# Reordering the prologue of a two-layer diffusion backbone: first modulation tile ahead of x, conditioning rows spread by TensorE, narrow products sooner

## The chip, the cores and the metric

The kernel runs on one core of one Trainium2 chip. The metric is the time of one execution on the device in microseconds, as the median of several runs. All data is fp32 unless said otherwise; "fp32r" is the form of fp32 operands for which TensorE needs one pass over the columns.

## The reference

512 tokens (256 context, 256 latent) of width 1024 go through two layers, each with a SwiGLU FFN, a token mixer and a second FFN. Ahead of each of these stands an adaptive norm. Only the first of them is touched by the change:

```python
s_lat = jax.nn.silu(c)                 # (1, 1024), conditioning of the latent tokens
s_ctx = jax.nn.silu(c_ctx)[None]       # (1, 1024), of the context tokens
m = s @ ada_w[l] + ada_b[l]            # 9 vectors of 1024: shift, scale, gate for three sub-layers
h = rms_norm(x, g) * (1 + scale) + shift
g, u = jnp.split(h @ w_in, 2, axis=-1)
y = (jax.nn.silu(g) * u) @ w_out
```

The scale and shift of the first norm are needed before the first product of the first FFN can run; every later modulation vector is made beside the FFN products.

## The kernel before

Tokens lie along the free axis: `x` is 128 partitions by 8 chunks (KD = 8) of the width by 512 tokens. A weight tile of 128x2048 is fetched raw, ScalarE copies its rounded half (`split_hi`, L463), VectorE subtracts to get the rest (`split_lo`, L684), and every product is three one-pass matmuls: low times high, high times low, high times high (`products`, L1025 to L1027). Each engine has one program written out in order; semaphores join them. SyncE (`sp_program`) issues the large loads on one queue, GpSimd (`pool_program`) the small tables and later the modulation tiles, ScalarE the first tables.

The prologue is what runs before the first FFN is in its stride. In the order of the code:

- SyncE issues the conditioning columns `c_cols` (8 KB), four loads of `x` (512 KB each, two chunks each), weight tile 0 (1 MB), `ada00` tile 0 (1 MB; tile k holds in its first half the weights of scale chunk k and in its second those of shift chunk k), `c_ctx` and `c` each broadcast to 128 partitions (512 KB each, into `silu_c`), `ada00` tile 1, weight tile 1, then `ada00` tiles 2 to 7.
- GpSimd waits for `ada00` tile 0, then issues eight small tables (semaphore `loaded`, 8 loads), then waits for `ada00` tile 7 and begins with the modulation tiles of the later norms.
- TensorE runs 20 filler matmuls on a zero tile (`idle`, 128x512 bf16, L1128), adds up the squares of x in four steps (L1289, two chunks each) with three fillers after each, spreads the inverse root over the partitions (`pe_rstd`, L1271), and enters `pe_first_pairs`. There `narrow(n, w)` multiplies tile n's scale (w = 0) or shift (w = 1) half by `c_cols`: 8 matmuls of 2 columns, 16 instructions (L1135). Chunk 0 takes both halves this way; for chunks 1 to 7 only the scale is made so (`scale(n)`), and the shift is made on VectorE by `dots(n)`: two multiply-and-sum instructions of 128x1024 (L947), one per stream.
- `main(k, s)` is the part of the first two output tiles (s = 0, 1) that chunk k of the normalised input gives: 6 matmuls of 128x512. From chunk 1 on TensorE's order is `main(k, 0)`, `main(k, 1)`, `scale(k + 2)`.
- ScalarE (`act_modulate`, `one(c)`) makes scale (L595) and shift (L599) of chunk c, applies them (L605, two streams) and rounds (L610). VectorE multiplies x by the inverse root (`rows`, L939) and makes the low half (`low`, L952).
- ScalarE needs a table of functions per kind. Before, it has the one for Sqrt loaded first and the one for Silu after the root of the first norm; Silu is next used at L475 in the first FFN.

## Time and profile before

| what | value |
|---|---|
| median of 3 runs | 2031.32 us |
| lowest, highest | 2025.6, 2032.45 us |
| span of the profiled execution (its own time, first to last instruction) | 2029.5 us |
| TensorE matmul busy | 1988.7 us, 98% |
| TensorE busy in the first 65 us | 62.46 us |
| mean granted TensorE clock, first 65 us | 0.89 |
| mean granted TensorE clock, whole span | 0.989 |
| share of the 16 DMA engines, first 65 us | 0.75 |

TensorE is busy nearly throughout, but in the prologue its busy time holds fillers, narrow matmuls whose time is their weight load, and stretches at half clock. The granted clock of 1 stands for 2.4 GHz, 0.5 for 1.2 GHz. The record of the clock begins at 1.00, but the fillers of the first microseconds stand 0.43 us apart, twice the 0.21 of later ones, so durations are the better witness there.

### The profile page before, as it was taken

To read this page: it belongs to the slowest core of one execution; us is meant where nothing else is said; L and a number is where in the kernel's file an instruction comes from. 1 tells how busy PE (TensorE), PEld (TensorE's weight loads), DVE (VectorE), ACT (ScalarE), POOL (GpSimd) and SP (SyncE) were. 2 spreads that over 40 slices of the span, in tenths; PEclk is the share of its full clock that TensorE was granted. 3 is DMA by queue.
4 is the path that set the end of the run, shared out by engine and by line. 5 is a ranking of instruction groups with operands and counts; after the bars stand their busy time and mean duration, and the time that the engine had idled before them with its cause. 6 is when DMAs were issued, how large, how long until landed. Compare 5 with 4: busy or idle time off the path is not lost.

```text
span 2029.5 us, 27640 instructions
## 1 busy us (share of the span) xinstructions
PE 1988.7 (98%) x10255; PEld 1686.5 (83%) x10255; DVE 1282.1 (63%) x1840; ACT 752.0 (37%) x990; POOL 109.0 (5%) x165
## 2 busy tenths in 40 slices
PE   9999999999999899999999999999999999989998
PEld 7888888896788889888888988888887888878886
DVE  6877577875647776877678753453346632656666
ACT  4422222345544334332122333212235432736453
POOL 1000000000003210000001000000000000000000
PEclk8999999999999999999999999999999999999999
DMA  9455555621220003555555532352234423043553
GB/s 350 165 184 179 176 188 173 198 94 42 83 73 21 1 11 115 192 181 182 177 184 169 180 125 96 101 176 96 68 127 147 151 97 104 21 161 135 177 191 124
DMA packets 52650, 274.80 MB, mean 135 GB/s; under 512 B 6128, under 2 KB 7472, under 8 KB 34256
## 3 DMA queue, kind: packets, MB, share of 16 engines
q1 hardware_dynamic: 33024, 203.97, 28.7%
q0 software_dynamic: 18960, 68.88, 10.2%
q8 instruction: 63, 1.03, 0.2%
q10 hardware_dynamic: 576, 0.69, 0.1%
q14 instruction: 27, 0.22, 0.0%
HBM read 272.47 MB, written 1.05 MB: 135 GB/s over the span
## 4 chain that ended last, share of the span: by engine, by line
PE 90%; DVE 4%; ACT 3%; DMA 1%; issue 1%; SPq 0%; DVEq 0%; ACTq 0%
PE ps L1025 15%; PE ps L1026 15%; PE ps L1027 15%; PE ps L1037 8%; PE ps L1255 6%; PE ps L1257 6%; PE ps L1256 6%; PE ps L1038 4%; PE ps L2402 2%; PE ps L2404 2%; PE ps L2403 2%; PE ps L1907 1%; DMA ada<-in_ada 1%; PE ps L1919 1%; PE ps L2488 1%
## 5 line engine op out<-in xcount | busy, mean ns | idle before, releaser
L684 DVE TENSOR_TENSOR w_lo<-w_raw,w_hi 128x2048 fp32r<-128x2048 f32 (+3 forms) x206 | 420.8, 2043 | 198.0 <-ACT w_hi L463 197.4
L1025 PE MATMUL ps<-h_parts,w_lo 128*128 128x512 f32 (+1 forms) x1424 | 537.5, 377 | 1.5 <-DVE w_lo L684 0.6
L1026 PE MATMUL ps<-h_parts,w_hi 128*128 128x512 f32 (+1 forms) x1424 | 534.9, 376 | 0.0
L1027 PE MATMUL ps<-h_parts,w_hi 128*128 128x512 f32 (+1 forms) x1424 | 534.9, 376 | 0.0
L463 ACT ACTIVATE w_hi<-w_raw 128x2048 fp32r<-128x2048 f32 (+3 forms) x207 | 354.0, 1710 | 444.8 <-PE ps L1257 254.0
L692 DVE SCALAR_TENSOR_TENSOR ada_product<-ada_w,silu_c 128x1024 bf16<-128x1024 f32 x256 | 313.2, 1224 | 20.4 <-DVE ada_product L692 10.3
L1025 PEld LDWEIGHTS ps<-h_parts,w_lo 128*128 128x128 f32 x1424 | 268.8, 189 | 51.2 <-DVE h_parts L2240 1.1
L1027 PEld LDWEIGHTS ps<-h_parts,w_hi 128*128 128x128 f32 x1424 | 268.8, 189 | 48.7
L1026 PEld LDWEIGHTS ps<-h_parts,w_hi 128*128 128x128 f32 x1424 | 268.8, 189 | 47.5
L475 ACT ACTIVATE sil<-ps 128x512 f32<-128x512 f32 x66 | 39.5, 598 | 481.1 <-PE ps L1027 481.1
L1255 PE MATMUL ps<-hid_parts,w_lo 128*128 128x512 f32 x468 | 182.1, 389 | 0.0
L1256 PE MATMUL ps<-hid_parts,w_hi 128*128 128x512 f32 x468 | 182.1, 389 | 0.0
L1257 PE MATMUL ps<-hid_parts,w_hi 128*128 128x512 f32 x468 | 182.1, 389 | 0.0
L717 DVE TENSOR_TENSOR prod<-sil,ps 128x512 f32<-128x512 f32 x66 | 45.4, 688 | 184.7 <-ACT sil L475 184.7
L1037 PE MATMUL ps<-h_parts,w_hi 128*128 128x512 f32 x416 | 149.0, 403 | 2.6 <-DVE h_parts L901 2.4
L755 DVE SCALAR_TENSOR_TENSOR x<-ps,mod,x 128x256 f32 (+1 forms) x144 | 65.4, 481 | 114.9 <-PE ps L1257 90.9
L428 POOL DMA_DIRECT2D ada_w<-in_ada x128 | 67.6, 529 | 964.3 <-DVE ada_product L692 936.3
L1038 PE MATMUL ps<-h_parts,w_lo 128*128 128x256 f32 x416 | 117.4, 282 | 0.0
L1257 PEld LDWEIGHTS ps<-hid_parts,w_hi 128*128 128x128 f32 x468 | 87.9, 188 | 18.3
L1256 PEld LDWEIGHTS ps<-hid_parts,w_hi 128*128 128x128 f32 x468 | 87.9, 188 | 18.2
L1255 PEld LDWEIGHTS ps<-hid_parts,w_lo 128*128 128x128 f32 x468 | 87.9, 188 | 18.2
L1037 PEld LDWEIGHTS ps<-h_parts,w_hi 128*128 128x128 f32 x416 | 79.4, 191 | 23.0 <-issue 2.6
(337 smaller groups left out, 2547.9 us busy)
## 6 DMA issues: line engine op xcount, KB each, us to landing
w_raw<-in_w_up SPq DMA_DIRECT2D x88, 1024.0 KB, 4.8
ada_w<-in_ada POOLq DMA_DIRECT2D x128, 512.0 KB, 3.5
w_raw<-in_w_down SPq DMA_DIRECT2D x32, 768.0 KB, 4.2
w_raw<-in_w_down SPq DMA_DIRECT2D x32, 640.0 KB, 3.9
w_raw<-in_w_ret_t SPq DMA_DIRECT2D x16, 1024.0 KB, 4.8
w_raw<-in_w_ab SPq DMA_DIRECT2D x14, 1024.0 KB, 4.7
ada<-in_ada SPq DMA_DIRECT2D x8, 1024.0 KB, 26.9
w_raw<-in_w_ret SPq DMA_DIRECT2D x8, 1024.0 KB, 4.7
```

Of the source, the lines that this page charges most:

```text
L428: pool.dma_start(ada_w[:, slot, :], a["ada"][bass.ds(index, 1)].rearrange("a p n -> (a p) n")) \
L463: act.activation(w_hi[parts_of(s, slot)][:, 0:elems], w_raw[slot][:, 0:elems], ACT.Copy).then_inc(hi_ready, 1)
L684: dve.tensor_tensor(w_lo[parts_of(s, slot)][:, 0:elems], w_raw[slot][:, 0:elems], w_hi[parts_of(s, slot)][:, 0:elems].bitcast(F32), ALU.su ...
L692: dve.scalar_tensor_tensor(out=ada_product[:], in0=ada_w[:, slot, :], scalar=1.0, in1=silu_c[:, st, :], op0=ALU.mult, op1=ALU.mult, accum_ ...
L1025: pe.matmul(out, lo, rhs_hi(k), start=first and k == 0, stop=False)
L1026: pe.matmul(out, hi, rhs_lo(k), start=False, stop=False)
L1027: mm = pe.matmul(out, hi, rhs_hi(k), start=False, stop=last and k == nk - 1)
L1037: pe.matmul(out, w_hi[slot][:, off:off + P], parts, start=start, stop=stop, skip_group_check=True)
L1038: return pe.matmul(out[:, LAT], w_lo[slot][:, off:off + P], parts[:, 1], start=False, stop=stop, skip_group_check=True)
L1255: pe.matmul(ps[:, 2 * slot, cols], wlo, hi, start=k == 0, stop=False)
L1256: pe.matmul(ps[:, 2 * slot, cols], whi, lo, start=False, stop=False)
L1257: mm = pe.matmul(ps[:, 2 * slot, cols], whi, hi, start=False, stop=k == nk - 1)
```

## The change

- SyncE: `ada00` tile 0 is issued ahead of the four loads of x; the two broadcasts of `c_ctx` and `c` go away.
- ScalarE: fetches `c_ctx` and `c` as rows of one partition (two loads, ahead of its tables), takes Silu of the columns and of the rows first, then squares, and runs the warm-up Sqrt after the squares.
- TensorE: 12 fillers, `narrow(0, 0)`, 3 fillers, `narrow(0, 1)`, 3 fillers ahead of the sums of squares; no filler between or after these. Four matmuls of 128x512 with a one-partition operand (`pe_spread_c`) spread the two Silu rows into PSUM banks 0 to 3: one before the third sum, one after the fourth, two after `pe_rstd`. VectorE copies the context row from PSUM into `silu_c`, ScalarE the latent row.
- The shift of chunk 1 is made by a narrow product too (`TURNED = 2`), so `dots` starts at chunk 2. The order in `pe_first_pairs` becomes `narrow(1, 0)`, `main(0, 0)`, `narrow(1, 1)`, `scale(2)`, `main(0, 1)`; its 14 fillers go away.
- VectorE: `low(0)` comes ahead of the copy, and later the order is `rows(c)`, `dots(c)`, `low(c - 1)`.
- GpSimd issues the small tables after `ada00` tile 6 instead of tile 0.

```diff
@@ sp_program
         sp.dma_start(c_cols, a["c_cols"]).then_inc(c_cols_loaded, 16)
+        scale_and_shift(0)
         for i in range(KD // 2):
             sp.dma_start(x[:, 2 * i:2 * i + 2], a["xT"][:, 2 * i:2 * i + 2]).then_inc(x_loaded[i], 16)
         weights(0)
-        scale_and_shift(0)
-        sp.dma_start(silu_c[:, 0, :], a["c_ctx"].partition_broadcast(P)).then_inc(c_loaded, 16)
-        sp.dma_start(silu_c[:, 1, :], a["c"][0, :].partition_broadcast(P)).then_inc(c_loaded, 16)
         scale_and_shift(1)
@@ pool_program
-        pool.wait_ge(ada00_ready[0], 16)
+        pool.wait_ge(ada00_ready[KD - 2], 16)
@@ act_modulate
-                if c:
-                    act.wait_ge(first_dot, 2 * c)
-                act.activation(mod[:, 0, 1, :, c], mcol[:, :, c] if c else ps[:, 5, 2:4], ACT.Identity,
+                if c >= TURNED:
+                    act.wait_ge(first_dot, 2 * (c - TURNED + 1))
+                act.activation(mod[:, 0, 1, :, c], ps[:, 5 + c % 2, 2:4] if c < TURNED else mcol[:, :, c], ACT.Identity,
...
                 if c == 0:
+                    act.wait_ge(c_spread, 2)
+                    act.activation(silu_c[:, 1, :].rearrange("p (b n) -> p b n", b=2), ps[:, 2:4, :], ACT.Copy) \
+                       .then_inc(c_spread_lat, 1)
                     split_hi(act, 1, 1, ELEMS[1])
@@ scalar_program
+        for st, row in enumerate((a["c_ctx"].unsqueeze(0), a["c"])):
+            act.dma_start(silu_c[0:1, st, :], row).then_inc(c_loaded, 16)
         act.dma_start(const[:, 0:2 * P], a["const"][:, 0:2 * P]).then_inc(const_loaded, 16)
...
-        act.wait_ge(sem("eps_set"), 1)
-        act.activation(warm_root[:], vecs[:, 2:3], ACT.Sqrt).then_inc(warmed, 1)
+        act.wait_ge(c_cols_loaded, 16)
+        act.activation(c_cols, c_cols, ACT.Silu).then_inc(c_silu, 1)
+        act.wait_ge(c_loaded, 32)
+        act.activation(silu_c[0:1], silu_c[0:1], ACT.Silu).then_inc(c_silu, 1)
         for r in range(0, KD, 2):
             act.wait_ge(x_loaded[r // 2], 16)
             act.activation(first_squares[:, r], x[:, r], ACT.Square).then_inc(even_squared, 1)
+        act.wait_ge(sem("eps_set"), 1)
+        act.activation(warm_root[:], vecs[:, 2:3], ACT.Sqrt).then_inc(warmed, 1)
         act_root(act, "n00", 0, 1.0 / D)
-        act.wait_ge(c_cols_loaded, 16)
-        act.activation(c_cols, c_cols, ACT.Silu).then_inc(c_silu, 1)
         split_hi(act, 0, 0, ELEMS[0])
-        act.wait_ge(c_loaded, 32)
-        act.activation(silu_c[:], silu_c[:], ACT.Silu).then_inc(c_silu, 1)
@@ vector_program
         rows(0)
+        split_lo(dve, 0, 0, ELEMS[0])
+        low(0)
+        dve.wait_ge(c_spread, 1)
+        dve.tensor_copy(silu_c[:, 0, :].rearrange("p (b n) -> p b n", b=2), ps[:, 0:2, :]).then_inc(c_spread_ctx, 1)
         rows(1)
-        split_lo(dve, 0, 0, ELEMS[0])
-        dve.wait_ge(c_silu, 2)
-        dots(1)
-        low(0)
         split_lo(dve, 1, 1, ELEMS[1])
-        for c in range(2, KD):
-            if c > 2:
-                dots(c)
-            low(c - 1)
-            if c == 2:
-                dots(c)
-            rows(c)
+        rows(2)
+        dve.wait_ge(c_spread_ctx, 1)
+        dots(2, (0,))
+        low(1)
+        dve.wait_ge(c_spread_lat, 1)
+        dots(2, (1,))
+        for c in range(3, KD):
+            rows(c)
+            dots(c)
+            low(c - 1)
@@ pe_spread_c, pe_first_pairs
+    def pe_spread_c(pe, st, half):
+        return pe.matmul(ps[:, 2 * st + half, :], one_column[0:1, 0:1].to_broadcast([1, P]),
+                         silu_c[0:1, st, half * 512:(half + 1) * 512], start=True, stop=True)
...
             if k == 0:
                 pe_ready(pe, s)
+                pe.wait_ge((c_spread_ctx, c_spread_lat)[s], 1)
...
-        narrow(0, 0)
-        idle(pe, 4)
-        narrow(0, 1).then_inc(scale_made, 1)
-        idle(pe, 4)
-        scale(1)
+        narrow(1, 0)
         main(0, 0)
-        idle(pe, 4)
+        narrow(1, 1).then_inc(scale_made, 1)
         scale(2)
-        idle(pe, 2)
         main(0, 1)
@@ tensor_program
-        idle(pe, 20)
+        idle(pe, 12)
+        pe.wait_ge(c_silu, 1)
+        pe_narrow(pe, 0, 0)
+        idle(pe, 3)
+        pe_narrow(pe, 0, 1).then_inc(scale_made, 1)
+        idle(pe, 3)
         for i in range(KD // 2):
+            if i == 2:
+                pe.wait_ge(c_silu, 2)
+                pe_spread_c(pe, 0, 0)
             pe.wait_ge(pair_summed, i + 1)
...
-            idle(pe, 3)
+        pe_spread_c(pe, 0, 1).then_inc(c_spread, 1)
         pe.wait_ge(const_loaded, 16)
         pe_rstd(pe, "n00", 0)
-        idle(pe, 3)
+        pe_spread_c(pe, 1, 0)
+        pe_spread_c(pe, 1, 1).then_inc(c_spread, 1)
```

The host side lays the shift half of `ada00` tile 1 out in columns like that of tile 0, at the same size.

## Rows read from the trace of the kernel before

**Rows 1.** The page's first line.

```profile
span 2029.5 us, 27640 instructions
```

**Rows 2.** The chain that ended last, first 70 us: shares by line; pieces (start, us, what).

```profile
by line: DMA ada<-in_ada 34.0%; PE ps L1135 14.8%; PE ps L1025 12.3%; PE ps L1026 11.0%; PE ps L1027 10.6%; SPq L387 2.5%; issue 1.7%; SPq L380 1.6%; ACT sil L605 1.6%; SPq L390 1.4%; SPq L383 1.4%; DVE h_parts L952 1.0%; DVE prod L717 1.0%
...
7.06 23.78 DMA ada<-in_ada
```

**Rows 3.** TensorE in order of time (start us, us, line, what, count).

```profile
1.48 7.02 PE L1128 MATMUL ps<-idle_tile 128*128 128x512 bf16 x20 [1.48 <-DVE idle_tile L923]
...
12.74 0.95 PE L1289 MATMUL ps<-one_column,first_squares 128*128 128x1 f32 x8
...
14.35 1.13 PE L1271 MATMUL ps<-const,small 128*128 128x128 f32 x8
...
15.96 1.85 PE L1135 MATMUL ps<-small,ada 128*128 128x2 f32 x16
...
22.56 3.57 PE L1135 MATMUL ps<-small,ada 128*128 128x2 f32 x16 [0.49 <-DMA ada<-in_ada]
...
28.71 1.93 PE L1128 MATMUL ps<-idle_tile 128*128 128x512 bf16 x4
30.89 1.95 PE L1135 MATMUL ps<-small,ada 128*128 128x2 f32 x16 [0.25 <-DMA ada<-in_ada]
...
32.93 0.58 PE L1025 MATMUL ps<-h_parts,w_lo 128*128 128x512 f32 x1
...
38.84 1.84 PE L1135 MATMUL ps<-small,ada 128*128 128x2 f32 x16
...
43.41 1.84 PE L1135 MATMUL ps<-small,ada 128*128 128x2 f32 x16
```

**Rows 4.** Two stretches: busy us by engine, granted clock (PEclk), DMA share, GB/s.

```profile
20.00:22.00 2.00, 2.00 (x8) 0.62 (x7) 0.00 (x0) 1.69 (x5) 0.43 (x1) 0.57 1.02 389
30.00:32.00 2.00, 1.75 (x12) 1.12 (x11) 2.00 (x3) 0.21 (x1) 0.00 (x0) 0.87 1.02 430
```

**Rows 5.** DMA issues of single stretches: KB, us from issue to landing.

```profile
x<-in_xT SPq DMA_DIRECT2D x1, 512.0 KB, 6.4
...
w_raw<-in_w_up SPq DMA_DIRECT2D x1, 1024.0 KB, 10.0
...
w_raw<-in_w_up SPq DMA_DIRECT2D x1, 1024.0 KB, 19.5
...
small<-in_lam POOLq DMA_DIRECT2D x1, 128.0 KB, 11.7
```

**Rows 6.** VectorE in order of time.

```profile
11.64 0.69 DVE L929 TENSOR_TENSOR first_squares<-first_squares 128x512 f32<-128x512 f32 x1
...
15.51 1.28 DVE L939 TENSOR_TENSOR prod<-x,ps 128x512 f32<-128x512 f32 x2 [1.26 <-PE ps L1271]
17.35 2.29 DVE L684 TENSOR_TENSOR w_lo<-w_raw,w_hi 128x2048 fp32r<-128x2048 f32 x1 [0.55 <-ACT w_hi L463]
```

**Rows 7.** ScalarE in order of time.

```profile
20.49 0.35 ACT L595 ACTIVATE mod<-ps,mod_tmp,norm_g 128x2 f32<-128x2 f32 x1 [0.27 <-PE ps L1135]
...
22.15 0.63 ACT L610 ACTIVATE h_parts<-sil 128x512 fp32r<-128x512 f32 x1
...
63.91 0.60 ACT L475 ACTIVATE sil<-ps 128x512 f32<-128x512 f32 x1 [2.53 <-PE ps L1027]
```

**Rows 8.** Later TensorE matmuls with two-pass fp32 operands of 512 columns.

```profile
479.28 1.13 PE L1405 MATMUL ps<-df 64*128 64x512 f32 x4
```

**Rows 9.** One line: a VectorE copy of 128x1024 from PSUM, ns min/median/max.

```profile
L2333 DVE COPY df<-ps x4: 1219/1222/1225, 425.0 to 452.5; 128x1024 f32<-128x1024 f32 x4
```

**Rows 10.** ScalarE later, a table load and the activation behind it.

```profile
527.00 1.28 ACT L1696 ACT_TABLE_LOAD   x1
531.22 0.31 ACT L1696 ACTIVATE small<-small,vecs 128x16 f32<-128x16 f32 x1 [2.94 <-DVE small L1700]
```

**Rows 11.** GpSimd in order of time.

```profile
43.71 1.06 POOL L428 DMA_DIRECT2D ada_w<-in_ada  x2 [23.28 <-DMA ada<-in_ada]
```

More of the change, by code:

```diff
@@ L939, in rows, with dots @@
             dve.tensor_tensor(prod[:, c % 2], x[:, c], ps[:, NRM, :], ALU.mult).then_inc(normed, 1)
-        def dots(c):
+        def dots(c, streams=range(2)):
             dve.wait_ge(ada00_ready[c], 16)
-            for st in range(2):
-                n = 2 * (c - 1) + st
+            for st in streams:
+                n = 2 * (c - TURNED) + st
                 if n:
@@ L1128, in idle, with pe_narrow @@
             pe.matmul(ps[:, 7, :], idle_tile[:, 0:P], idle_tile[:], start=True, stop=True)
+    def pe_narrow(pe, n, w):
+        if w == 0:
+            pe.wait_ge(ada00_ready[n], 16)
+        for k in range(KD):
+            mm = pe.matmul(ps[:, 5 + n % 2, 2 * w:2 * w + 2], first_weights(n)[:, w, k * P:(k + 1) * P],
+                           c_cols[:, 2 * k:2 * k + 2], start=k == 0 and w == 0, stop=k == KD - 1,
+                           skip_group_check=True)
+        return mm
+    def pe_spread_c(pe, st, half):
+        return pe.matmul(ps[:, 2 * st + half, :], one_column[0:1, 0:1].to_broadcast([1, P]),
+                         silu_c[0:1, st, half * 512:(half + 1) * 512], start=True, stop=True)
     def pe_first_pairs(pe):
         def narrow(n, w):
-            for k in range(KD):
-                mm = pe.matmul(ps[:, 5 + n % 2, 2 * w:2 * w + 2], first_weights(n)[:, w, k * P:(k + 1) * P],
-                               c_cols[:, 2 * k:2 * k + 2], start=k == 0 and w == 0, stop=k == KD - 1,
-                               skip_group_check=True)
-            return mm
+            return pe_narrow(pe, n, w)
         def scale(n):
-            pe.wait_ge(ada00_ready[n], 16)
-            if n >= 2:
-                pe.wait_ge(first_mod, n - 1)
+            pe.wait_ge(first_mod, n - 1)
             narrow(n, 0).then_inc(scale_made, 1)
```

8 lines of the change are left out of this document (4 added, 4 removed).

## Prediction

> **What bounds the kernel now.** The page gives a span of 2029.5 us [rows 1]; the median of the runs is 2031.32 us, 1.8 us more. I make the sum on the profiled execution and subtract the result from the median. The runs shown scatter over 6.9 us (2025.6 to 2032.45), so 0.3% (6.1 us) is about what a measurement can tell from no change.
>
> I read the chain of waits first. In its first 70 us the largest share, 34%, is one transfer: `ada00` tile 2, issued at 7.06 and landed 23.78 us later, at 30.85 [rows 2]. `scale(2)` starts on TensorE right then, at 30.89 [rows 3]. Next I read TensorE in order of time. After `scale(2)` come `main(0, 1)` at 32.93, then 18 matmuls of 128x512 in all, then `scale(3)` at 38.84. From there on a period of 4.57 us (38.84 to 43.41) repeats with hardly a gap [rows 3]: 16 instructions of a narrow product and 12 wide matmuls. So the prologue is bound by a transfer up to 30.9 us and by TensorE's own work after it. Whatever brings the start of `scale(3)` forward brings the end forward by the same, because the work behind it is unchanged. **38.84 us is the mark to beat.**
>
> The third thing to see is the clock. The same 16 instructions of a narrow product take 1.85 us at 15.96 and 3.57 us at 22.56; four fillers take 1.93 us at 28.71 (0.43 each), where 12 cold and 8 warm ones fill the first 7.02 us: 12 x 0.43 = 5.1, 8 x 0.21 = 1.7 and the tail of the last [rows 3]. The granted clock agrees: its mean over 20 to 22 us is 0.57, so it fell to 0.5 early in that stretch, and over 30 to 32 us it is 0.87, so it came back [rows 4]. It fell after two narrow products with four fillers between; it came back after 6 wide matmuls and 4 fillers in a row. Prices below are written "at 2.4 | at 1.2 GHz".
>
> **The change, part by part.** *Ahead of the sums.* Twelve fillers from 1.48 last 12 x 0.43 = 5.1, to 6.6. Then TensorE waits for `ada00` tile 0. It is now the first megabyte of the queue. Before, the first megabyte was the first two loads of x; the second of them was issued at about 1.8 and landed 6.4 later, at 8.2 [rows 5]. The start therefore lies between 6.6 and 8.2; I take the middle, 7.4. ScalarE's Silu of the columns (a table load of 1.28 [rows 10], and a few tenths) is done by about 5, under the fillers. Two narrow products at 1.84 and six fillers at 0.21 make 5.0, so the sums can start at 12.4.
>
> *Sums of squares and spreads.* x lies a megabyte later in the queue. Its last load now ends where weight tile 0's third megabyte ended: issued 3.29, landed 10.0 later, 13.3 [rows 5]. VectorE then needs two passes of 0.69 [rows 6], to 14.7, which is before TensorE reaches the fourth sum. So TensorE is late, not x: four sums at about 1.0 (0.95 busy [rows 3]), with one spread in between. The trace has no matmul of 512 columns with one partition. From below it is bounded by the one-pass wide matmul, 0.23; from above by the two-pass fp32 matmuls of 512 columns over half the rows, four instructions in 1.13 [rows 8], if none of them overlap, 0.57 for two. The two-pass instructions of 512 columns at filler rate give 4 x 0.21 = 0.85 if each instruction streams its columns twice, and this is the bound I take, since it is the dearest. Sums end at 12.4 + 4.0 + 0.85 = 17.3. Before they ended at 12.74 + 0.95 = 13.7 [rows 3]: 3.6 later. The next spread (0.85) hides root and inverse, which took 0.7 between 13.7 and 14.35; then `pe_rstd` takes 1.1 [rows 3], to 19.3 (before 15.5).
>
> *Up to `main(0, 0)`.* VectorE: `rows(0)` 0.64, `split_lo` 2.29 [rows 6], by then ScalarE has rounded chunk 0 (20.49 to 22.78, 2.3 in all [rows 7], here 19.9 to 22.2), `low(0)` 0.69, and the new copy from PSUM 1.22 [rows 9]. That is 4.9 with the small overlaps: 24.2. TensorE meanwhile does two spreads and `narrow(1, 0)`: 19.3 + 1.7 + 1.84 = 22.8, covered; if VectorE's 4.9 were gone, it would be the bound 1.4 earlier. The copy is on the path, since `main(0, 0)` writes the banks it reads. Before, `main(0, 0)` started behind the narrow product of 22.56, at 26.1 [rows 3].
>
> *Up to `main(0, 1)`.* Six matmuls 1.4 | 2.6 and two narrow products 3.7 | 6.9 [rows 3]: 5.1 | 9.5, so 29.3 | 33.7. The same kinds of work ran mostly at 1.2 GHz in the stretch this replaces. I take the middle, 31.5, against 32.93. Tile 2 is now the seventh megabyte; the seventh before, weight tile 1, was issued at 6.59 and landed 19.5 later, at 26.1 [rows 5], and it had the small tables beside it, which are now moved behind. `scale(2)` asks for it at 27.4 at the earliest, so it is no longer waited for. ScalarE's copy (about 1.1) and split of weight tile 1 and VectorE's part of it end near 27.5, covered.
>
> *Up to `scale(3)`.* 18 matmuls: 4.2 all at 2.4 GHz; before 38.84 - 32.93 = 5.9, part of it at 1.2. I take 5.9: 31.5 + 5.9 = 37.4. **Sum: 38.84 - 37.4 = 1.4 us gained.** At the fast ends 29.3 + 4.2 = 33.5, a gain of 5.3; VectorE's new order (copy, `rows(1)`, `split_lo(1)`, `rows(2)`, `dots(2)`, `low(1)`, `rows(3)`, `dots(3)`, `low(2)`) reaches 35.4 there, when TensorE has done `scale(3)` at 35.3, so it does not cut this. At the slow ends 33.7 + 5.9 = 39.6, a loss of 0.8.
>
> *Edits costed at nothing.* `dots(1)` leaves VectorE, 2.5 us that did not set the end. VectorE's work per chunk, 0.65 + 2.5 + 0.69 = 3.8, stays under TensorE's 4.57. GpSimd's tables: even if issued from 43.7 [rows 11], eight at 0.54 and the slowest landing of 11.7 [rows 5] give 59.7, before the end of the last chunk at about 62; their real start is tile 6, earlier. If that margin went, all three engines would stand at `loaded`. The modulation tiles queue behind them on GpSimd by 4.3 us; nothing reads them before the first FFN. The third table load: Silu's table must come back before L475. A table load ran ahead of its activation's wait at 527.00 (end 528.28, then 2.94 idle [rows 10]), and L475 has 2.53 of idle [rows 7], so 1.28 is hidden; unhidden it costs 1.3.
>
> The Trainium skill, "ScalarE: Activation LUTs", section "What ACT_TABLE_LOAD costs", puts a switch at about 2.66 us with its drain. The trace shows 1.28 and an activation right behind; by the page the load at L475 would stick out of its cover by 0.1 us.
>
> **The rivals.** *B, the clock falls in the first narrow products and stays down through the sums.* For it: the pair narrow, fillers, narrow is what stood ahead of the fall at 20 us, and now there are 3 fillers instead of 4 between, a wait ahead of it, and none between the sums. Against it: the sums before, with three fillers after each, and the narrow product at 15.96 behind them ran at the prices of 2.4 GHz [rows 3], and the spreads are dense work in the fillers' place. Price, with narrow's ratio 3.57/1.85 for work set by weight loads: fillers 0.65, sums 4 x 0.9 = 3.7, two spreads 1.7, `pe_rstd` 0.9: 7.0, so `pe_rstd` ends at 26.3, and TensorE's two spreads and `narrow(1, 0)` at 1.2 GHz (3.4 + 3.4) end at 33.1, past VectorE. Then 5.1 | 9.5 and 5.9 give 44.1 to 48.5: 5.3 to 9.7 slower, **2036.6 to 2041.0 us**. It decides the sign as soon as it costs over 1.4 us, that is from two cold sums on, and passes 0.3% at 7.5.
>
> The Trainium skill, "TensorE: Matmul & The Clock Gate", section "What's actually happening", says that the array is throttled by default and that activity releases it; the rows of the clock agree, and by this rule leaving 18 of the 49 fillers speaks for B.
>
> *C, the queue is no faster.* If tile 2 still lands at 30.9, because the large loads and not the small tables slowed the queue, `scale(2)` ends at 32.7 and `main(0, 1)` starts 0.2 earlier: **2031.1 us**. For it: the DMA engines are full (share 1.02) in both stretches [rows 4]. Against it: the queue carries one megabyte less ahead of tile 2.
>
> *D, the clock holds throughout:* gain 5.3, **2026.0 us**. For it: the sums' stretch before. Against it: the narrow products do not hold it.
>
> **How the numbers follow.** The forecast (A, partly cold) gets 0.47, B 0.22, C 0.13, D 0.12, and 0.06 is for what lies elsewhere. A: 2031.32 - 1.4 = **2029.9 us**, its own range 2026 to 2032. The range over all is 2025.0 to 2039.0: from D's 2026.0 with a microsecond of scatter to the middle of B; outside are B's upper part and scatter. Faster by over 0.3% needs D and scatter: 0.08. Slower by over 0.3%: three quarters of B, and a little for the rest: 0.18. Within: 0.74.
>
> **What the profile after would show.** The first narrow product at 6.6 to 8.2 us; sums ending near 17.3, `pe_rstd` near 19.3, a copy of 1.22 on VectorE ending just ahead of `main(0, 0)` near 24.2; `scale(2)` without a wait for DMA; `scale(3)` near 37.4; a table load inside the idle time ahead of L475. B shows as narrow products of 3.4 us or sums of 1.8 before 20 us and a granted clock of 0.5 there. C shows as a DMA wait at `scale(2)`. If the spreads take far from 0.85 each, or the first tile lands after 8.2, that term is wrong; if `scale(3)` moves and the span doesn't, the step that carries the prologue's gain to the end is.

## The result and the profile after

The changed kernel takes 2042.29 us, the median of 9 runs from 2036.9 to 2043.4. The kernel before, run 9 times beside it, takes 2026.62 us (2022.69 to 2032.45). The ratio is 1.0061 with a 95% interval of 1.0049 to 1.0073. The two medians alone differ by 15.7 us (0.77%), the ratio stands for 12.3 us; the ratio with its interval is what is used from here on. The change makes the kernel slower by about 0.6%, and the time lies above the stated range, though the kernel before turned out 4.7 us faster in nine runs than in the three that the forecast was subtracted from. One execution of the kernel before, in the group of experiment 10, took 6544.77 us and is left out of the ratios. The profiled execution took 2042.18 us.

The page's first line stands against [rows 1]: the span grew by 10.9 us.

```profile
span 2040.4 us, 27627 instructions
```

The chain of waits of the changed kernel, its first pieces (start us, us, what), answers to [rows 2]. The one long transfer is gone. From 6.71 us on, with hardly a gap, every piece up to the first FFN is TensorE.

```profile
1.34 5.24 DMA ada<-in_ada
6.71 1.98 PE ps L1144 x16
8.70 1.30 PE ps L1136 x3
10.00 3.20 PE ps L1144 x16
13.20 1.30 PE ps L1136 x3
14.51 3.21 PE ps L1306 x16
17.71 2.00 PE ps L1150 x2
19.71 3.50 PE ps L1306 x16
23.21 2.00 PE ps L1150 x2
25.21 2.00 PE ps L1280 x8
27.21 3.71 PE ps L1150 x4
30.92 3.50 PE ps L1144 x16
```

In the changed file L1144 is the narrow product, L1136 a filler, L1306 the sum of squares, L1150 the spread of a conditioning row, L1280 `pe_rstd`, and L1033 to L1035 the three wide matmuls. Two instructions of L1150 are one spread and 16 of L1306 are two sums.

TensorE of the changed kernel in order of time, behind the last piece above, answers to [rows 3]. The 16 instructions at 50.53 are `scale(3)`, which started at 38.84 before: **11.7 us later**. The one at 78.36 is the first of the third weight tile, which started at 65.38 before: 13.0 us later.

```profile
34.28 0.77 PE L1033 MATMUL ps<-h_parts,w_lo 128*128 128x512 f32 x1
...
36.99 6.82 PE L1144 MATMUL ps<-small,ada 128*128 128x2 f32 x32
43.67 0.77 PE L1033 MATMUL ps<-h_parts,w_lo 128*128 128x512 f32 x1
...
50.53 1.84 PE L1144 MATMUL ps<-small,ada 128*128 128x2 f32 x16
...
55.10 1.84 PE L1144 MATMUL ps<-small,ada 128*128 128x2 f32 x16
...
78.36 0.47 PE L1033 MATMUL ps<-h_parts,w_lo 128*128 128x512 f32 x1 [1.46 <-DVE prod L722]
```

The clock, with the columns of [rows 4]: it falls in the stretch from 8 us (1.00 from 6 to 8, then 0.61, then 0.50) and comes back in the one from 48 us, so about 41 us of the prologue run at 1.2 GHz. In half-microsecond stretches the fall is at 8.4 us, while the very first narrow product ends.

```profile
8.00:10.00 2.00, 2.00 (x11) 1.36 (x10) 1.53 (x3) 0.80 (x2) 0.00 (x0) 0.61 1.04 410
10.00:12.00 2.00, 2.00 (x12) 2.00 (x11) 1.93 (x4) 1.09 (x2) 0.00 (x0) 0.50 1.10 444
...
48.00:50.00 2.00, 2.00 (x7) 1.54 (x6) 2.00 (x4) 0.00 (x0) 0.00 (x0) 0.65 0.00 0
```

ScalarE answers to [rows 7, 10]. Its third table load stands behind the release of L475, not inside the idle time ahead of it.

```profile
75.60 1.28 ACT L475 ACT_TABLE_LOAD   x1 [2.53 <-PE ps L1035]
76.90 0.60 ACT L475 ACTIVATE sil<-ps 128x512 f32<-128x512 f32 x1
```

From 11.7 to 13.0 us later, this load accounts for the step of 1.3. Behind that point the changed kernel's span is 2040.4 - 78.36 = 1962.0 us, that of before 2029.5 - 65.38 = 1964.1. 13.0 - 2.1 is the 10.9 of the spans. Nothing in the change touches that part, and the profiles of all versions scatter there from 1958.7 to 1966.0 us, so the 2.1 is within what one execution differs from the next. The granted clock dips in this part too, in every version, near 620 to 660 and 1820 to 1860 us among others.

### The profile page after: what moved, and what is told of

It is laid out like the page before. It is cut to its first block, busy times and chain, and to the rows that moved or that the text cites. A ratio compares the mean times of both kernels' runs of the same rounds, so it can differ in the third digit from the quotient of the medians.

```text
span 2040.4 us, 27627 instructions
## 1 busy us (share of the span) xinstructions
PE 1998.4 (98%) x10248; PEld 1696.0 (83%) x10248; DVE 1280.9 (63%) x1837; ACT 754.0 (37%) x992; POOL 109.0 (5%) x165
## 3 DMA queue, kind: packets, MB, share of 16 engines
HBM read 271.43 MB, written 1.05 MB: 134 GB/s over the span
## 4 chain that ended last, share of the span: by engine, by line
PE 92%; DVE 4%; ACT 3%; issue 1%; DMA 0%; DVEq 0%; ACTq 0%; SPq 0%
PE ps L1033 15%; PE ps L1034 15%; PE ps L1035 15%; PE ps L1045 7%; PE ps L1265 6%; PE ps L1264 6%; PE ps L1266 6%; PE ps L1046 4%; PE ps L2420 2%; PE ps L2422 2%; PE ps L2421 2%; PE ps L1144 1%; PE ps L1925 1%; PE ps L1937 1%; PE ps L2506 1%; PE ps L1933 1%
## 5 line engine op out<-in xcount | busy, mean ns | idle before, releaser
L1033 PE MATMUL ps<-h_parts,w_lo 128*128 128x512 f32 (+1 forms) x1424 | 538.0, 378 | 2.8 <-DVE prod L722 1.5
L1035 PE MATMUL ps<-h_parts,w_hi 128*128 128x512 f32 (+1 forms) x1424 | 535.2, 376 | 0.0
L1033 PEld LDWEIGHTS ps<-h_parts,w_lo 128*128 128x128 f32 x1424 | 269.1, 189 | 52.7 <-issue 1.9
L1035 PEld LDWEIGHTS ps<-h_parts,w_hi 128*128 128x128 f32 x1424 | 268.9, 189 | 48.6
L475 ACT ACTIVATE sil<-ps 128x512 f32<-128x512 f32 x66 | 39.5, 598 | 478.7 <-PE ps L1035 478.7
L1264 PEld LDWEIGHTS ps<-hid_parts,w_lo 128*128 128x128 f32 x468 | 87.8, 188 | 18.4
L1266 PEld LDWEIGHTS ps<-hid_parts,w_hi 128*128 128x128 f32 x468 | 87.8, 188 | 18.2
```

Of the source, the lines that this page charges most:

```text
L1033: pe.matmul(out, lo, rhs_hi(k), start=first and k == 0, stop=False)
L1035: mm = pe.matmul(out, hi, rhs_hi(k), start=False, stop=last and k == nk - 1)
L1264: pe.matmul(ps[:, 2 * slot, cols], wlo, hi, start=k == 0, stop=False)
L1266: mm = pe.matmul(ps[:, 2 * slot, cols], whi, hi, start=False, stop=k == nk - 1)
```

## The experiments

Medians of the kernel before in the five groups of runs were 2030.60, 2026.97, 2027.42, 2026.33 and 2028.16 us. Each ratio below is against the runs of its own group. "Mark" is the start of `scale(3)` in the profiled execution: 38.84 before, 50.53 after. The mark is one execution, the ratio many. Where the two disagree, both are told. Where a time is given for the fall or the return of the clock, it comes from the granted clock in stretches of half a microsecond or of two.

**1. Only the fillers of the changed kernel, in the kernel before.**

```diff
-        idle(pe, 20)
+        idle(pe, 12)
...
             mm.then_inc(ssq_done, 1)
-            idle(pe, 3)
...
         narrow(0, 0)
-        idle(pe, 4)
+        idle(pe, 3)
         narrow(0, 1).then_inc(scale_made, 1)
-        idle(pe, 4)
+        idle(pe, 3)
...
         main(0, 0)
-        idle(pe, 4)
         scale(2)
-        idle(pe, 2)
```

> The kernel before with only its fillers cut to the count and pattern of the changed kernel (12 at the start, 3 after each narrow product of chunk 0, none after the sums, the root's spread or in the first pairs). Theory F (the lost clock is the whole cost, and it is lost because the fillers went): TensorE falls to 1.2 GHz within the first 16 us and stays there up to the wide matmuls; the sums take 1.7 us each, the start of scale(3) moves from 38.8 to 43 us or later; ratio 1.002 to 1.005. Rival O (the new order of work costs, not the fillers): ratio 1.000 within 0.001, the clock as before.

Measured: 2030.69 us, ratio 1.0002 [0.999, 1.0013]. The stretches of the clock:

```profile
10.00:12.00 2.00, 2.00 (x10) 2.00 (x10) 1.15 (x2) 0.31 (x1) 0.00 (x0) 0.50 0.99 418
...
36.00:38.00 2.00, 2.00 (x8) 1.54 (x8) 2.00 (x4) 0.90 (x2) 0.00 (x0) 0.71 0.99 418
```

31 of the 49 fillers are gone, and the clock is at 1.2 GHz from 9.9 to 37.2 us. `main(0, 0)` starts at 28.27, 2.3 us later than before, but `scale(2)` at 30.98 against 30.89, and the mark is at 39.81, only 1.0 us later. In the kernel before TensorE waits for the queue up to 30.9 us anyway, and that wait takes up most of what the clock costs. So the fillers matter for the clock, but taking them out of the kernel before is not what costs 12 us.

**2. The fillers of before put back in the changed kernel**, the reverse of the diff above, with three fillers behind each sum.

> The changed kernel with the fillers of before put back in the places that still exist (20 at the start, 4 after each narrow product of chunk 0, 3 after the four sums and after the root's spread, 4 after main(0, 0), 2 after scale(2)). Theory F: the clock holds 2.4 GHz through most of the sums, scale(3) starts at 36 to 42 us instead of 50.5, ratio to the kernel before 0.999 to 1.003. Rival N (the pair of narrow products ahead of the sums drops the clock whatever fillers stand round it): the clock falls near 9 to 13 us as in the changed kernel, scale(3) starts at 50 us or later, ratio 1.006 or more.

Measured: 2044.52 us, ratio 1.0073 [1.0046, 1.0099], the mark at 51.55. Nothing is won.

```profile
10.00:12.00 2.00, 2.00 (x19) 1.85 (x18) 1.96 (x4) 1.22 (x2) 0.00 (x0) 1.00 1.05 426
12.00:14.00 2.00, 1.93 (x9) 1.28 (x9) 1.93 (x4) 1.33 (x3) 0.00 (x0) 0.59 1.05 436
```

The clock now outlasts both narrow products and falls at 12.4 us. It comes back at 32.8, within a pair of one-partition spreads, falls again at 36.2 and is up once more from 39.7 to 43.1 us.

```profile
32.38 2.19 PE L1150 MATMUL ps<-silu_c,one_column 1*128 1x512 f32 x4
```

What this gives back (the two spreads in 2.19 us instead of 3.78) is less than the fillers cost: `main(0, 0)` starts 2.2 us later than in the changed kernel. The missing fillers are not the cause of the loss.

**3. Only the small tables later, in the kernel before.**

```diff
-        pool.wait_ge(ada00_ready[0], 16)
+        pool.wait_ge(ada00_ready[KD - 2], 16)
```

> The kernel before with one line of the change: the small tables are issued after ada00 tile 6. Theory (the small packets slowed the queue ahead of tile 2): tile 2 lands at 26 to 29 us instead of 30.9, and TensorE, which waited for it, starts scale(3) 1 to 3 us earlier; ratio 0.9985 to 0.9995. Rival C (the large loads alone set the queue): tile 2 lands at 30.9 within 0.5, ratio 1.000.

Measured: 2026.11 us, ratio 0.9989 [0.9976, 1.0002]. Tile 2, issued at 7.1, landed 19.3 us later at 26.4, against 30.85 before; the mark is at 35.18, 3.7 earlier. The same once more:

> before_tables_last once more, beside it and in more rounds: scale(3) at 35 to 37 us, ratio 0.9985 to 0.9995 with an interval that leaves 1 out; the rival is that its gain does not show in the time.

Measured: 2026.49 us, ratio 0.9991 [0.9979, 1.0003], tile 2 19.2 us after its issue, the mark at 34.67. Both intervals just touch 1. In these two profiles of one and the same kernel the clock fell at 18.2 and at 24.7 us: where it falls differs from execution to execution. The step from the small tables to a faster queue holds. It is worth about 0.1%, less than the 3.7 to 4.2 us of the mark in these two profiles would say.

**4. Silu's table fetched in ScalarE's free time**, in the changed kernel.

```diff
         act_modulate(act, "n00")
+        act.activation(warm_root[:], vecs[:, 2:3], ACT.Silu).then_inc(warmed, 1)
```

> The changed kernel with a Silu of one column put behind the last modulation of the first norm on ScalarE, so that the table load stands ahead of the wait for the first product. Theory: the load of 1.28 us runs in the 2.5 us of idle, the wait of TensorE ahead of the third weight tile falls from 1.46 to 0.2 us, the time falls by 1.3 us (ratio to the changed kernel 0.9994). Rival: something else (VectorE) held that wait, and nothing moves.

Measured: 2041.96 us, ratio 1.0066 [1.0043, 1.0089]. The load now runs earlier and the activation at L475 right at its release; TensorE's wait for the product behind it is 0.20 instead of 1.46.

```profile
71.36 1.28 ACT L658 ACT_TABLE_LOAD   x1
...
73.88 0.60 ACT L475 ACTIVATE sil<-ps 128x512 f32<-128x512 f32 x1 [1.02 <-PE ps L1036]
```

The trace shows the 1.26 us gone from the path. In the times it is within the scatter of the runs.

**5. Chunk 0's narrow products behind `pe_rstd`, with the fillers of before**, in the changed kernel.

```diff
-        idle(pe, 12)
-        pe.wait_ge(c_silu, 1)
-        pe_narrow(pe, 0, 0)
-        idle(pe, 3)
-        pe_narrow(pe, 0, 1).then_inc(scale_made, 1)
-        idle(pe, 3)
+        idle(pe, 20)
...
             mm.then_inc(ssq_done, 1)
+            idle(pe, 3)
...
         pe_rstd(pe, "n00", 0)
+        pe.wait_ge(c_silu, 1)
+        pe_narrow(pe, 0, 0)
+        idle(pe, 4)
+        pe_narrow(pe, 0, 1).then_inc(scale_made, 1)
+        idle(pe, 4)
```

> The changed kernel with both narrow products of chunk 0 moved behind the root's spread (where they stood before, 4 fillers after each), 20 fillers at the start and 3 after each of the four sums. Theory N (the narrow products ahead of the sums both lengthen the chain by 5 us and drop the clock for all behind them): the sums run at 2.4 GHz and end at 14 to 16 us instead of 23.2, the root's spread ends by 18, scale(3) starts at 39 to 43 us instead of 50.5, ratio to the kernel before 1.000 to 1.003. Rival S (the four spreads of the conditioning rows are the cost): scale(3) stays at 46 us or later.

Measured: 2051.02 us, ratio 1.012 [1.0103, 1.0137], the mark at 58.42: slower than the changed kernel by another 0.6%. So the new place of the narrow products isn't by itself what costs: with the old one the clock falls as well, at 13.0 us. TensorE's rows show what stands around the fall.

```profile
10.01 1.05 PE L1301 MATMUL ps<-one_column,first_squares 128*128 128x1 f32 x8 [1.71 <-DVE first_squares L934]
...
12.38 0.81 PE L1136 MATMUL ps<-idle_tile 128*128 128x512 bf16 x3
13.12 2.07 PE L1150 MATMUL ps<-silu_c,one_column 1*128 1x512 f32 x2
15.12 1.87 PE L1301 MATMUL ps<-one_column,first_squares 128*128 128x1 f32 x8
```

The fillers at 12.38 have the price of 2.4 GHz, the first spread already that of 1.2 GHz, and the sum behind it takes 1.87 us against 0.95 in [rows 3]. The spread began at 13.12 us, when the clock had just gone down, so it can't be what brought it down here; a wait of 1.71 us for the squares stood ahead of the fall. What the spreads may do is keep the clock down: it stayed low until 57.4 us. Experiments 9 and 10 put that to the test.

**6. A filler behind every narrow matmul of tiles 0 to 2, and three behind each sum**, in the changed kernel.

```diff
                            skip_group_check=True)
+            if k < KD - 1:
+                idle(pe, fill)
         return mm
```

> The changed kernel with one filler behind every matmul of the narrow products of chunks 0 to 2 (7 more per product) and 3 behind each sum: order and dependences as in the changed kernel, 54 more fillers. Theory F' (with enough dense work in between the clock holds, and a held clock is worth more than the fillers cost): 2.4 GHz from 6 us on, sums of 1.0 us, spreads of 0.9 us, scale(3) at 40 to 44 us, ratio 1.001 to 1.004. Rival: the clock falls in the narrow products all the same, each of them now takes over 6 us at 1.2 GHz, scale(3) at 55 us or later, ratio 1.008 or more.

Measured: 2040.42 us, ratio 1.006 [1.0043, 1.0077], the mark at 48.16. The clock holds through both narrow products, although TensorE had waited 1.20 us for tile 0 just ahead of them, and through the first two sums. So it is the narrow products without fillers within, and not the wait, that stand for the early fall in the changed kernel. Then comes the first spread, still at the price of 2.4 GHz, and the clock falls behind it, at 18.4 us.

```profile
16.61 1.12 PE L1152 MATMUL ps<-silu_c,one_column 1*128 1x512 f32 x2
```

```profile
18.00:20.00 2.00, 2.00 (x10) 1.36 (x10) 0.00 (x0) 0.00 (x0) 0.00 (x0) 0.59 0.99 401
```

The first fence is TensorE in order of time, the second a stretch of the clock; it came back at 38.9 us. The mark is 2.4 us earlier than in the changed kernel, yet this execution's span is 1.4 us longer (2041.8), because it lost 3.8 us behind the prologue.

**7. The rows by two DMA broadcasts as before, all else as changed.** No spreads, no copies from PSUM. ScalarE's Silu of the rows, now of 128 partitions, moves behind the modulation of chunk 0.

```diff
         weights(0)
+        sp.dma_start(silu_c[:, 0, :], a["c_ctx"].partition_broadcast(P)).then_inc(c_loaded, 16)
+        sp.dma_start(silu_c[:, 1, :], a["c"][0, :].partition_broadcast(P)).then_inc(c_loaded, 16)
...
-            if i == 2:
-                pe.wait_ge(c_silu, 2)
-                pe_spread_c(pe, 0, 0)
-        pe_spread_c(pe, 0, 1).then_inc(c_spread, 1)
...
-        pe_spread_c(pe, 1, 0)
-        pe_spread_c(pe, 1, 1).then_inc(c_spread, 1)
```

> The changed kernel with the conditioning rows fetched as before by two broadcasts of 512 KB behind weight tile 0; no spreads by TensorE and no copies from PSUM. Theory (the spreads run at 1.2 GHz, 2.0 us each, two of them ahead of the root's spread, and the copy of 1.22 us stands ahead of main(0, 0)): main(0, 0) starts 5 us earlier, scale(3) at 44 to 46 us instead of 50.5, ratio to the kernel before 1.002 to 1.004. Rival (the DMA queue's extra megabyte gives it back): TensorE waits for ada00 tile 1 or 2 and scale(3) stays past 48.

Measured: 2033.53 us over 10 runs (2030.1 to 2037.6), ratio 1.0029 [1.0014, 1.0044]: the spreads and what goes with them are 0.0061 - 0.0029 = 0.0032, 6.5 us of the 12.3. Some 1.3 of this isn't theirs: with Silu of the rows in its new place, Silu's table is loaded there and no longer at L475.

```profile
25.97 1.28 ACT L621 ACT_TABLE_LOAD   x1
```

In the profiled execution, at 2030.19 us the fast end of these runs, the mark is at 39.17, 11.4 us earlier than in the changed kernel.

```profile
13.22 6.83 PE L1296 MATMUL ps<-one_column,first_squares 128*128 128x1 f32 x32
...
26.82 0.77 PE L1027 MATMUL ps<-h_parts,w_lo 128*128 128x512 f32 x1 [0.86 <-DVE h_parts L954]
```

The four sums still run at 1.2 GHz (6.83 us, against 3.8 at the 0.95 each of [rows 3]), but `main(0, 0)` starts at 26.8 instead of 34.3. So 7.5 of the 11.4 us are won up to `main(0, 0)`, about what the four spreads themselves take at 1.2 GHz (2.00 + 2.00 + 3.71 in the chain of waits). The other 3.9 are won behind it, with the clock back at 2.4 GHz from 30.1 to 33.5 and from 36.9 us on, where the changed kernel has it from 49.4.

**8. The rest of the change: rows by DMA, chunk 0's narrow products behind `pe_rstd`, fillers around the sums, Silu's table early** (experiments 4, 5 and 7 in one). What remains is tile 0 first, tables last and the new order of `pe_first_pairs` with `TURNED = 2` and no fillers in it.

> The rest of the change without the work that it put on TensorE's path: tile 0 ahead of x, small tables last, both halves of chunk 1 by narrow products in the new order, rows by DMA broadcast, chunk 0's narrow products behind the root's spread, 20 fillers at the start, 3 per sum, 4 after each narrow product of chunk 0, none in the first pairs. Theory: the queue is no bound, TensorE is, the sums end at 14 to 15 us; scale(3) at 36 to 40 us, ratio 0.998 to 1.001. Rival (the order of the first pairs costs by itself, 3 narrow products in a row at 1.2 GHz): scale(3) at 42 us or later, ratio 1.002 or more.

Measured: 2035.43 us (2029.1 to 2040.0), ratio 1.0035 [1.0022, 1.0048], the mark at 40.66. Against experiment 3, which has the faster queue too, the mark is 5.5 to 6.0 us later. Up to `main(0, 0)`, at 25.75 us, it is 0.8 to 1.3 later, with x a megabyte later in the queue; between `main(0, 0)` and `main(0, 1)` it loses 3.5 (9.38 us against 5.9). The clock holds to 20.9 us, then falls and stays down to about 38. `narrow(1, 1)` and `scale(2)` then stand in one row at 1.2 GHz:

```profile
28.45 6.82 PE L1139 MATMUL ps<-small,ada 128*128 128x2 f32 x32
```

The same with four fillers behind `main(0, 0)`:

```diff
         main(0, 0)
+        idle(pe, 4)
         narrow(1, 1).then_inc(scale_made, 1)
         scale(2)
```

> tables_last_turned_two with 4 fillers put back behind main(0, 0). Theory (three narrow products at 1.2 GHz, the last two 6.8 us, are what the new order of the first pairs costs, because the dense stretch that brought the clock back was taken out): the clock is back at 2.4 GHz by 30 to 31 us, the two narrow products take 3.7 to 5 us, scale(3) at 38 to 40 us instead of 40.7, ratio 1.001 to 1.003. Rival: the clock does not come back, the fillers add 1.7 us, scale(3) at 42 us or later.

Measured: 2036.91 us (2030.7 to 2040.9), ratio 1.0039 [1.0022, 1.0055]. In its profile the clock fell at about 11 us already, behind a wait of 2.33 us for squares of x, and the mark is at 46.31. So it doesn't say what the four fillers do. But it says something else. Up to the first product of `main(0, 0)` the two kernels are the same instruction for instruction, and that product starts at 25.75 us in the one profile and at 31.44 in the other: 5.7 us between two executions of the same work, with the clock's fall at 20.9 and at 11.1 us.

**9. One spread behind each sum, of one partition or of 128, in the kernel before.** The spread replaces the three fillers and writes a bank that nobody reads. The two variants are alike in every other respect.

```diff
             mm.then_inc(ssq_done, 1)
-            idle(pe, 3)
+            pe.matmul(ps[:, 7, :], one_column[0:R, 0:1].to_broadcast([R, P]), x[0:R, 0, :], start=True, stop=True)
```

> The kernel before with the 3 fillers behind each of the four sums replaced by one spread-like matmul (fp32, 512 columns, an operand of one partition, into an unused bank; it adds nothing to the result). Theory R (a one-partition matmul does not hold the clock, though TensorE is as busy with it as with a full one): the clock falls to 1.2 GHz at 10 to 14 us, the later of these matmuls take 2.0 us each; scale(3) 1 to 3 us later than 38.8. Rival: it holds the clock as the fillers did, up to about 20 us.

> The same with the same two-pass matmul over all 128 partitions. Theory R: it holds the clock, 1.0 us each, and the clock falls only near 20 us behind the narrow products, as in the kernel before. Rival (the number of partitions does not matter, or the fp32 kind does not hold it): the same fall as with one partition.

With R = 1, one run of 2037.4 us, TensorE and then the stretches:

```profile
8.90 1.12 PE L1292 MATMUL ps<-x,one_column 1*128 1x512 f32 x2
...
10.94 1.12 PE L1292 MATMUL ps<-x,one_column 1*128 1x512 f32 x2
...
13.04 2.07 PE L1292 MATMUL ps<-x,one_column 1*128 1x512 f32 x2
```

```profile
12.00:14.00 2.00, 2.00 (x10) 1.52 (x10) 0.00 (x0) 0.00 (x0) 0.00 (x0) 0.71 1.00 406
```

With R = 128, one run of 2028.04 us:

```profile
12.10 1.10 PE L1292 MATMUL ps<-x,one_column 128*128 128x512 f32 x2
...
13.85 1.10 PE L1292 MATMUL ps<-x,one_column 128*128 128x512 f32 x2
```

```profile
12.00:14.00 2.00, 2.00 (x14) 1.52 (x14) 0.00 (x0) 0.00 (x0) 0.00 (x0) 1.00 0.98 397
...
22.00:24.00 2.00, 1.83 (x12) 1.75 (x12) 1.85 (x3) 1.12 (x2) 0.00 (x0) 0.65 1.04 428
```

At 2.4 GHz both cost nearly the same (1.12 and 1.10 us; from start to the next start 1.06 and 0.94), and TensorE is busy throughout the sums in both. With one partition the clock falls at 12.8 us and comes back at 40.1; with 128 it holds to 22.6. The marks are 46.10 and 38.68: **7.4 us between two kernels that differ only in the number of partitions**, and 9.4 between the two times. This is one execution of each, and the place of the fall moves by itself, by 6.5 us in experiment 3 and 9.8 in experiment 8, so the pair alone doesn't prove it. For it speaks that no other profile that has the sums ahead of the narrow products, with fillers or full spreads between them, and no long wait (1.71 us or more) ahead of the first sum shows the clock down before 18 us. Experiment 10 has more executions.

**10. The changed kernel with spreads over 128 partitions.** The other 127 rows are zero; the two conditioning rows land in other buffers.

```diff
-        return pe.matmul(ps[:, 2 * st + half, :], one_column[0:1, 0:1].to_broadcast([1, P]),
-                         silu_c[0:1, st, half * 512:(half + 1) * 512], start=True, stop=True)
+        return pe.matmul(ps[:, 2 * st + half, :], one_column[:, 0:1].to_broadcast([P, P]),
+                         silu_c[:, st, half * 512:(half + 1) * 512], start=True, stop=True)
...
+        dve.memset(silu_c[:], 0.0).then_inc(sem("c_zeroed"), 1)
```

> The changed kernel with its four spreads over all 128 partitions: silu_c is zeroed first, the rows land in another tile and their Silu is written into partition 0, so the sum over 128 partitions gives the same row. Nothing else moves. Theory R (one-partition spreads keep the clock down in the changed kernel too): the clock has already fallen at the first narrow pair near 9 us, but comes back within the dense spreads (before 30 us at the latest), scale(3) at 43 to 48 us instead of 50.5, ratio to the kernel before 1.002 to 1.005. Rival (once it has fallen in the narrow products the kind of spread does not matter): clock and times as in the changed kernel, scale(3) within 1 us of 50.5.

Measured: 2037.98 us, ratio 1.005 [1.0031, 1.007], the mark at 45.97, 4.6 earlier than in the changed kernel.

```profile
26.00:28.00 2.00, 2.00 (x9) 1.10 (x7) 2.00 (x2) 1.60 (x4) 0.00 (x0) 0.86 1.03 418
```

The clock, down since 9.5 us, comes back in the two full spreads behind `pe_rstd` (the four instructions take 2.55 us instead of 3.78) and falls again at about 30, in the narrow products, to 43.6. The gain isn't clear of noise in the times: the intervals of the two ratios overlap, and the profiled execution, the slowest of its four, has a span only 0.6 us shorter than the changed kernel's, since it is 4.0 longer behind the prologue. The same edit on experiment 5:

> after_narrow0_behind (narrow products of chunk 0 behind the root's spread, fillers in the sums; scale(3) at 58.4, ratio 1.012) with the spreads over all 128 partitions. Theory R: the clock, which fell at 13.5 us with the first one-partition spread, holds through the sums and to the narrow products (20 us or later); scale(3) at 44 to 50 us, ratio 1.004 to 1.007. Rival: the clock falls at 13 to 14 us again, scale(3) stays past 56.

Measured: 2039.1 us, ratio 1.0066 [1.0046, 1.0087], against 1.012 with one partition; the mark at 48.14 against 58.42. Here the times are plain: four executions of 2036.5 to 2042.7 us against four of 2050.4 to 2052.7.

```profile
10.37 1.05 PE L1304 MATMUL ps<-one_column,first_squares 128*128 128x1 f32 x8 [2.64 <-DVE first_squares L937]
```

Here the clock fell at 12 us, behind a wait of 2.64 us for the squares, and came back at about 25.5, behind a full spread and `pe_rstd`. So it fell early with either kind of spread; what differs is that with full spreads it comes back some 30 us sooner, though it falls twice more (29.0 to 35.8, 43.1 to 46.0). Full spreads do not make the order of the change fast.

**11. From the queue's side: tables last in the kernel before, without its eight fillers around chunk 0's narrow products.**

```diff
         narrow(0, 0)
-        idle(pe, 4)
         narrow(0, 1).then_inc(scale_made, 1)
-        idle(pe, 4)
```

> The kernel before with the small tables last and without the 8 fillers around chunk 0's narrow products. With the tables last TensorE, not the queue, sets the prologue from 15 us on. Theory: the fillers there did not keep the clock up (it fell near 19 to 20 us with them) and only cost 0.85 and 1.5 us, so scale(3) starts at 32.5 to 35 us, ratio 0.997 to 0.999. Rival (without them the clock falls before both narrow products): scale(3) at 35.5 us or later, ratio 0.9985 to 1.000.

Measured: 2027.03 us, ratio 0.9994 [0.9985, 1.0004]; the clock fell at about 19.3 us, the mark is at 35.38.

```profile
20.90 3.57 PE L1135 MATMUL ps<-small,ada 128*128 128x2 f32 x16 [1.82 <-DMA ada<-in_ada]
```

`scale(1)` waited 1.82 us for its tile ahead of its 3.57: again half the clock costs little where a transfer is late.

**12. Tables last, and one filler behind each narrow matmul of tiles 0 and 1** in place of those eight.

```diff
                                skip_group_check=True)
+                if n < 2 and k < KD - 1:
+                    idle(pe, 1)
```

> The kernel before with the small tables last and one filler behind every matmul of the narrow products of chunks 0 and 1 (21 in all), in place of the 8 around chunk 0's. Theory (dense work within the narrow products holds the clock, and with the queue out of the way a held clock shortens the path): 2.4 GHz up to the first wide matmuls at 23 us, the wide matmuls of main(0, 0) take 1.4 instead of 2.6 us, scale(3) at 31.5 to 34.5 us (35.2 with the tables last alone), ratio 0.997 to 0.999. Rival: the 21 fillers cost as much as the clock gives back, scale(3) within 0.7 us of 35.2.

Measured: 2024.44 us over 12 runs (2021.4 to 2030.6), ratio 0.9987 [0.9977, 0.9998], the mark at 33.28, the earliest of all.

```profile
24.00:26.00 2.00, 1.41 (x7) 1.06 (x7) 0.89 (x2) 2.00 (x3) 0.00 (x0) 1.00 0.99 418
```

```profile
24.69 0.47 PE L1025 MATMUL ps<-h_parts,w_lo 128*128 128x512 f32 x1 [0.59 <-DVE h_parts L952]
```

The granted clock is 1.00 in all stretches from 16 to 34 us, and `main(0, 0)` waits for VectorE. The interval just leaves 1 out: of all versions this is the only one for which a gain on the kernel before is shown.

## Why the prediction was wrong

**The step that failed** is the pricing of TensorE's work ahead of `main(0, 0)` at 2.4 GHz: the narrow pair at 1.84 each, the sums at 1.0, the spreads at 0.85, on the ground that "the spreads are dense work in the fillers' place". In the changed kernel the clock is down as the first narrow product ends, at 8.4 us, and all of TensorE's work from there to 49 us is at 1.2 GHz; with fillers within the narrow products it holds there (experiment 6). A spread takes 1.05 us at 2.4 and 2.0 at 1.2 GHz, and one-partition spreads don't do for the clock what full ones do: over all 128 partitions they bring it back at 26.6 us, for 3.4 us at first, instead of 49.4 in the changed kernel, and 32 us sooner in experiment 5's (experiment 10), and of the pair in experiment 9 the one with a single partition loses it first. That isn't a rule without exception, since in experiment 2 the clock came back within one-partition spreads. The prediction's bound from above for a spread, 0.57 by [rows 8], doesn't hold either.

Term by term, as the prediction put it, with what the profile after shows:

| term | predicted | measured |
|---|---|---|
| first narrow product starts | 7.4 | 6.71 |
| narrow pair and fillers | 5.0 | 7.6, sums from 14.30 |
| four sums and one spread | 4.85 | 8.9, end 23.2 |
| spread and `pe_rstd` | 2.0, end 19.3 | 4.0, end 27.2 |
| to `main(0, 0)` | VectorE 4.9, 24.2 | TensorE 7.1 (two spreads, `narrow(1, 0)`), 34.28 |
| to `main(0, 1)` | 7.3 (5.1 to 9.5), 31.5 | 9.4, 43.67 |
| to `scale(3)` | 5.9, 37.4 | 6.86, 50.53 |

The second thing that turned over is which engine bounds the part up to `main(0, 0)`. The prediction had VectorE there, with its copy on the path. In the trace VectorE's copy ends before TensorE is through:

```profile
30.44 0.69 DVE L957 TENSOR_TENSOR h_parts<-sil,h_parts 128x512 fp32r<-128x512 f32 x1 [0.30 <-ACT h_parts L610]
31.05 1.22 DVE L963 COPY silu_c<-ps 128x1024 f32<-128x1024 f32 x1
```

It is done at 32.3, and `main(0, 0)` starts behind TensorE's own work at 34.28. The 1.22 itself was right.

**Rival B** named the mechanism, the clock down from the first narrow products through the sums, and had a chance of 0.22. It too was mis-sized: at most 9.7 us at the mark, where 11.7 were measured. B's dearest case has `main(0, 0)` at 33.1 and `scale(3)` at 48.5; measured are 34.28 and 50.53. Up to `main(0, 0)` the narrow pair and its fillers are 1.9 more (7.6 against 5.65, since B left the second narrow product at 1.84 and slowed half the fillers) and the four spreads 0.9 more (7.7 against 6.8), less 0.7 for the earlier start and 0.8 for the sums (6.9 against 7.7): about the 1.2 there. The last 18 matmuls are 1.0 more (6.86 against 5.9). And one of B's grounds, only 18 of the 49 fillers left, was not the cause of the loss (experiments 1 and 2). The rule of the Trainium skill, "TensorE: Matmul & The Clock Gate", section "What's actually happening", that activity releases the throttle, is borne out by the clock's return behind rows of wide matmuls; but in experiment 9 the clock fell while TensorE was busy without a gap, and that measurement decides.

**Why the clock costs so much here and so little in experiment 1.** Before, TensorE had idle time ahead of 30.9 us because of the queue, and work at half speed filled it. The change does remove that wait, and the prediction was right there: tile 2, now issued at 5.76, landed 16.6 us later at 22.4, and `scale(2)` waits for no DMA. But it also puts four spreads in front of `main(0, 0)` and a narrow product more in front of `main(0, 1)`, so that TensorE's own work is the path from 6.7 us on, and what the clock adds to each piece of it (16 instructions of a narrow product 3.41 instead of 1.84) is added to the end. What the queue won (3.7 to 4.2 at the mark by itself, experiment 3) is hidden under this.

**The table load at L475** was costed at nothing, 1.28 inside 2.53 of idle time, by the example of [rows 10]. It ran behind the wait and cost its whole 1.28; experiment 4 moved it and took TensorE's wait from 1.46 to 0.20. The prediction had this as its unhidden price of 1.3.

**What was right:** the DMA side (first tile earlier than taken, x's last load at 12.4 for 13.3, the tables' later start without a stall at `loaded`), the copy, and the step that carries the mark to the end of the kernel. Rival C (no faster queue) and rival D (clock holds) both fell.

**How the loss is made up.** By the ratios, experiment 7 gives back 6.5 of 12.3 us, of which 1.3 are the table load and some 5 the spreads; by the two profiles it gives back 11.4 of 11.7 at the mark, but that of experiment 7 is a fast one among its runs. The rest, 0.3%, lies in what experiment 7 keeps of the change: narrow products ahead of the sums and three narrow products nearly in a row in `pe_first_pairs`. Experiment 8 has the old place for chunk 0's pair and still reads 1.0035, and it loses 3.5 us between `main(0, 0)` and `main(0, 1)`, so the new order of the first pairs, with x later, is argued to be the larger part of it; no run has changed that order alone.

**What stays open.** Several variants of the change scatter over 6 to 11 us between runs. The mean granted clock of every execution is known, and the slower ones of a kernel are those with the lower clock: of the changed kernel's nine, three take 2036.9 to 2038.6 us at 0.986 to 0.987 and six 2042.2 to 2043.4 at 0.983, and over 85 executions of the kernel before the two go together with a correlation of -0.87. In which stretch an execution lost its clock only a profile shows, so how much of this lies in the prologue is open, and with it why the same instructions find the clock falling at 11 us one time and at 21 another. How the last 0.3% splits was not settled. Why one table load runs ahead of a wait and another behind wasn't tried.

## What to carry to other kernels

Before work is moved to TensorE because it is "free", look at what TensorE waits for at that place: filling a wait is cheap at either clock, work on the path is paid at the clock that it leaves behind. Don't count on a matmul with one partition as a filler: spread it over all 128 with zeros, or leave a row's broadcast to a DMA. Where narrow matmuls must stand in a row, one dense filler behind each held the clock where four between two groups didn't; in the kernel before this was tried only together with earlier transfers, and there it paid. Read the clock of more than one execution before you explain a few microseconds by where it fell.

## What the runs showed of the hardware

- Two-pass fp32 matmuls of 512 columns take nearly the same time with one partition as with 128 (1.12 and 1.10 us at 2.4 GHz), but the clock fell at 12.8 us with the one and held to 22.6 with the other (one execution each). With the spreads of experiment 5 over 128 partitions instead of one, four executions took 2036.5 to 2042.7 us instead of 2050.4 to 2052.7.
- At 1.2 GHz the 16 instructions of a narrow product take 3.41 to 3.57 us instead of 1.84, nearly the factor of a filler of 512 columns (0.43 and 0.21).
- A wait of 1.7 to 2.6 us ahead of the first sum stood ahead of a fall of the clock at 11 to 13 us in three kernels (experiments 5, 8 and 10). Without such a wait the same instructions as in experiment 8's kept it to 20.9 us.
- Eight small tables issued beside the large queue made a 1 MB tile land 4.5 us later (30.85 against 26.4).
- A table load of 1.28 us ran in the idle time ahead of its activation in one place [rows 10] and behind the release in another (75.60).
